# Token-row projections: the moving operand and the output of their matmuls walked in runs of 16 columns, alternately from two halves

## Time and profile before

| | |
|---|---|
| time before, median of 3 | 1237.65 us (1237.44 to 1240.28) |
| the profiled execution's own time | 1240.36 us |
| its span, first to last instruction | 1238.5 us |
| PE busy, matmuls | 1207.6 us (98%), 7597 |
| PE weight loads busy | 1015.8 us (82%) |
| DVE, ACT, POOL busy | 902.3, 638.7, 102.3 us |
| mean granted TensorE clock | 0.998 of full speed |

### The profile page before, as it was taken

One profiled execution on the slowest core, in us unless ns is written; L12 is line 12 of the kernel. 1 busy time (PEld: TensorE's weight loads), 2 busy tenths in 40 slices (PEclk: granted clock), 3 DMA queues, 4 the chain that ended last, 5 costly groups with the idle time before them and its releaser, 6 DMA issues.

```text
span 1238.5 us, 19034 instructions
## 1 busy us (share of the span) xinstructions
PE 1207.6 (98%) x7597; PEld 1015.8 (82%) x7597; DVE 902.3 (73%) x1463; ACT 638.7 (52%) x1034; POOL 102.3 (8%) x163
## 2 busy tenths in 40 slices
PE   7999999999999999999999999999999999999998
PEld 3566778887978888787999987988788787999986
DVE  7998867767598998687656555589998687665553
ACT  4334565575547665546434443556575535444441
POOL 6400011101000200201000001000200201000000
PEclk9999999999999999999999999999999999999999
DMA  7735566444565455355666664565445355556552
GB/s 253 210 103 178 200 210 191 152 130 154 162 202 166 151 160 188 124 179 170 208 187 187 187 190 155 174 217 171 154 153 180 139 174 170 188 195 196 191 194 75
DMA packets 71958, 215.68 MB, mean 174 GB/s; under 512 B 16256, under 2 KB 19744, under 8 KB 71744
## 3 DMA queue, kind: packets, MB, share of 16 engines
q1 hardware_dynamic: 65008, 206.37, 52.0%
q0 software_dynamic: 2112, 6.97, 1.9%
q10 hardware_dynamic: 4752, 1.14, 0.4%
HBM read 208.95 MB, written 3.15 MB: 171 GB/s over the span
## 4 chain that ended last, share of the span: by engine, by line
PE 82%; DVE 10%; ACT 5%; issue 2%; POOL 1%; DMA 0%; SPq 0%; DVEq 0%; POOLq 0%; ACTq 0%
PE acc L705 16%; PE acc L706 16%; PE acc L707 16%; PE acc L683 7%; PE acc L684 7%; PE acc L685 7%; PE acc L642 3%; DVE weights_lo L1780 2%; PE mixed L1020 1%; ACT junk L1284 1%; PE mixed L1117 1%; PE turned L760 1%; ACT weights_hi L1249 1%; DVE h_T L1810 1%; PE mixed L1004 1%
## 5 line engine op out<-in xcount | busy, mean ns | idle before, releaser
L1780 DVE TENSOR_TENSOR weights_lo<-weights_raw,weights_hi 128x1024 fp32r<-128x1024 f32 (+1 forms) x304 | 356.1, 1206 | 67.2 <-ACT weights_hi L1249 66.3
L1249 ACT ACTIVATE weights_hi<-weights_raw 128x1024 fp32r<-128x1024 f32 (+1 forms) x304 | 305.6, 1043 | 77.2 <-DMA weights_raw<-stream_dram 77.0
L705 PE MATMUL acc<-weights_hi,act_F_hi 128*128 128x512 f32 (+1 forms) x656 | 264.8, 404 | 4.2 <-DVE weights_lo L1780 2.5
L707 PE MATMUL acc<-weights_hi,act_F_lo 128*128 128x512 f32 (+1 forms) x656 | 256.7, 391 | 0.0
L706 PE MATMUL acc<-weights_lo,act_F_hi 128*128 128x512 f32 (+1 forms) x656 | 256.5, 391 | 0.0
L683 PE MATMUL acc<-act_F_hi,weights_hi 128*128 128x256 f32 x624 | 175.1, 281 | 0.0
L684 PE MATMUL acc<-act_F_hi,weights_lo 128*128 128x256 f32 x624 | 173.9, 279 | 0.0
L685 PE MATMUL acc<-act_F_lo,weights_hi 128*128 128x256 f32 x624 | 173.9, 279 | 0.0
L705 PEld LDWEIGHTS acc<-weights_hi,act_F_hi 128*128 128x128 f32 x656 | 123.6, 188 | 32.6 <-DVE weights_lo L1780 3.6
L707 PEld LDWEIGHTS acc<-weights_hi,act_F_lo 128*128 128x128 f32 x656 | 123.4, 188 | 26.8
L706 PEld LDWEIGHTS acc<-weights_lo,act_F_hi 128*128 128x128 f32 x656 | 123.7, 189 | 24.0
(11 more groups left out here) (351 smaller groups left out, 1969.6 us busy)
## 6 DMA issues: line engine op xcount, KB each, us to landing
weights_raw<-stream_dram SPq DMA_DIRECT2D x306, 512.0 KB, 3.6
weights_raw_more<-stream_dram SPq DMA_DIRECT2D x58, 512.0 KB, 3.6
gains<-rows_dram POOLq DMA_DIRECT2D x12, 512.0 KB, 4.7
weights_raw<-stream_dram SPq DMA_DIRECT2D x6, 416.0 KB, 3.1
weights_raw<-stream_dram SPq DMA_DIRECT2D x4, 384.0 KB, 3.9
x_T<-x_in_dram SPq DMA_DIRECT2D x4, 256.0 KB, 6.4
ssm_bc<-ssm_bc_dram SPq DMA_DIRECT2D x1, 1024.0 KB, 8.1
u_scratch<-u_T ACTq DMA_DIRECT2D x4, 256.0 KB, 6.2
```

Source lines behind the costliest of these rows:

```text
L705: pe.matmul(o, xh, wh, start=first and kk == 0, stop=False)
L707: i = pe.matmul(o, xl, wh, start=False, stop=last and kk == s["nk"] - 1)
L1249: act.activation(high(s, slice(0, n)), whole(s, slice(0, n)), ACT.Copy).then_inc(hi_made, 1)
L1780: dve.tensor_tensor(low(s, slice(0, n)), whole(s, slice(0, n)), high(s, slice(0, n)).bitcast(F32), ALU.subtract).then_inc(lo_made, 1)
```

## The change

In `tile_slot` the moving operands `wh` and `wl` and the output `o` get another access pattern, for all three matmuls. The w columns are seen as two halves (h) of n runs of 16 columns (c), and the order becomes n, h, c. For w = 512 TensorE is fed columns 0 to 15, 256 to 271, 16 to 31, 272 to 287, and so on, and writes each product column to the same column of PSUM as before. For w = 416 and 384 the halves are 208 and 192 columns wide. Data in memory, results and the instruction lists stay as they are otherwise.

```diff
@@ -702,6 +702,7 @@ def tile_slot(at, t):
                     wh, wl = (f(at, slice(kk * w, (kk + 1) * w)) for f in (high, low))
                     xh, xl = (f[:, k, t * P:(t + 1) * P] for f in (hi, lo))
                     o = acc[par][t][:, 0:w]
+                    wh, wl, o = (x.rearrange("p (h n c) -> p n h c", h=2, c=16) for x in (wh, wl, o))
                     pe.matmul(o, xh, wh, start=first and kk == 0, stop=False)
                     pe.matmul(o, xh, wl, start=False, stop=False)
                     i = pe.matmul(o, xl, wh, start=False, stop=last and kk == s["nk"] - 1)
```

## The result

The changed kernel is slower: median 1264.85 us (1263.36 to 1267.05, 4 runs) against 1237.73 us, ratio 1.022, interval 1.0208 to 1.0233. The forecast of no change (1237.7 us) was wrong by 27 us; the range, 1234 to 1278 us, held the time, and 0.32 had been given to slower. The profiled execution took 1265.93 us, with a span of 1264.1 against 1238.5: 25.6 us more.

What follows compares the result with a forecast made beforehand. The prediction took TensorE (PE) to bound the kernel. With zero added for reading and for writing in runs, the profiled execution stays at 1240.36 us, in terms of the median 1237.7 us; range 1234 to 1278 us.

Steps and rivals of the forecast that it cites:

- What bounds the kernel: TensorE, busy 98% of the span; a cost added to the touched matmuls arrives with a factor of 0.85 to 1.
- Writing in runs: PSUM side of the touched matmuls: taken as zero, assumed to behave like the reading side; no row shows it.
- rival 2: PSUM writes lose two columns' time or more per jump: 67 to 79 us, 1305 to 1317 us or above; chance 0.09.
- Reading in runs: Moving operands of the touched matmuls: taken as zero from line 900; 0.42 ns per jump kept for the range.
- Rival 1: Touched matmuls: each jump costs one column's time, at full rate only; 39.6 us of PE, 1271 to 1277 us; chance 0.14.
- Rival 3: Touched matmuls: a jump costs under 0.18 ns, which line 900 can't show; up to 17 us, 1242 to 1255 us; chance 0.09.
- Rival 4: Touched matmuls: the fixed 15 ns shrink to 2.6 ns; 34 to 40 us less, 1198 to 1204 us; chance 0.06 with parts.
- Rival 5: Touched matmuls' pattern is merged to the old one, time as forecast; counted within no change's 0.62.
- The range: Whole kernel, 1234 to 1278 us: the likeliest case, Rival 3 and Rival 1; rival 2 and nearly all of Rival 4 left out.

Runs made afterwards that it cites:

- e9: Kernel before, but the plain float32 matmuls in `whole_slot` (line 642) read and write in runs of 16 from the two halves; 1238.1 us, ratio 0.9994.
- e2: Kernel before, but only the output is written in runs of 16 to the two halves, reading in one piece; 1237.72 us, ratio 1.0001.
- e8: Kernel before, but only the output is written in pairs of columns, in turn to the two halves; 1239.26 us, ratio 1.0019.

## Why the prediction failed where it did

- *What bounds the kernel* was right: of the engines' busy times only PE's and its weight loads' changed, and 0.85 of PE's added time reached the median (27.1 of 31.8 us), at the lower end of the 0.85 to 1 expected.
- *Writing in runs* costs zero: right, and now shown for runs of 16 and of 2. No row stood behind it; it was an assumption that came true. So rival 2, the loss on the write side, is out. The Trainium skill's page "PSUM — Partial Sum Buffer" (section "Specifications (TRN2)") says that any non-contiguous pattern slows matmuls significantly; on this side the runs do not agree. They are in line with a sentence of the Trainium skill's page "Advanced Engine Details and Errata" (section "PSUM Cachelines"), which asks that every two consecutive elements be contiguous; writing single columns, the case that would test it, was not run.
- *Reading in runs* at zero is the step that failed: it cost 10.4 ns for each matmul with 512 columns. The zero was taken from line 900, which walks 8 runs of 16 for nothing, but at plain float32's rate. The text named this gap (room to hide 0.42 ns per jump) and then took the row's value all the same. e9 shows that plain float32 is no witness: the very same 31 jumps cost nothing in it, at 0.84 ns a column, and 10.4 ns in the touched lines, at 0.42.
- *Rival 1* (a price per jump at the full rate only) had the place and the condition right, and the size near: 10.4 / 31 = 0.34 ns per jump instead of 0.42, 1264.85 us instead of 1271 to 1277. Its law was wrong: with 512 columns 3 jumps cost nothing, 15 cost 0.47 ns each, 127 cost 0.17 each. So that the time came near its 1271 us is in part luck: at 31 jumps the price happened to lie near one column's time. Rival 3's bound of 0.18 ns, taken from line 900, was passed at the change's own 31 jumps.
- *Rival 4* was given little because "Nothing in the rows supports that the order of columns enters there", into the 15 ns. The order does enter: single columns in turn reduce them to 2.5 ns, near float32's 2.6, in 1208 us. In the changed kernel it did not come.
- *Rival 5*, a pattern merged to the old one, is out by the distances alone.
- *The range* held because the gap of the reading row had been carried into it as 34 to 40 us; 27 came. That is a hedge that held; the mechanism behind the likeliest value, reading for nothing, was wrong.

## What to carry to other kernels

A row that shows an access pattern for nothing vouches for it only at its own rate and in its own type: ask whether the row ran slow enough to hide the cost, and weigh that gap in the likeliest value, not only in the range. Where the same matmul runs thousands of times on a bound engine, take its distance from start to start less its columns; what is left may belong to how the operand is read. Here, at one column per 0.417 ns, a moving operand of 512 columns was as fast in runs of 128 as in one piece (229.6 ns), slower in runs of 4 to 32 (236.7 to 250.7 ns) and fastest in single columns (215.8 ns); an output written in runs of 16 or in pairs cost nothing.

## What the runs showed that was not expected

- Reading single columns in turn from two places 256 columns apart is faster than reading neighbours: 215.8 against 229.6 ns. Whether that comes from a step other than one between neighbours or from the distance, and why runs of 4 to 32 are worse than both ends, stays open; no run tells it apart. Runs of 2 were not read.
- Single distances differ in their evenness. In the kernel before, dense neighbours with 512 columns were 225 to 237 ns apart, in many stretches 226, 229 and 232 over and over; in the changed kernel 2733 of 2778 were 240 exactly, and with single columns all but one were 215 or 216. So the 15 ns are a mean, not a constant.
- The traces speak against other traffic as the cause of those 15 ns. Before, the distance was 229.0 ns where DVE and ACT were each idle for at least half of it and 229.7 where both were busy for more than half; with fewer than four DMA transfers under way it was 229.6, with 16 or more 229.4.
- The mean cost is on a grid for three run lengths: 568, 576 and 584 columns' times with 512 columns for runs of 32, 16 and 8 (236.7, 240.0, 243.4 ns times 2.4), and 424, 432 and 440 with 384 columns (176.9, 180.1, 183.3 ns). Runs of 4 leave it (250.7 ns is 602 with 512 columns, 188.4 ns is 452 with 384).
- The untouched lines 683 to 685 come in two distances. Two stretches of the kernel before, each 24 matmuls long:

```profile
699.84 0.28 PE L683 MATMUL acc<-act_F_hi,weights_hi_more 128*128 128x256 f32 x1
...
702.66 0.28 PE L683 MATMUL acc<-act_F_hi,weights_hi_more 128*128 128x256 f32 x1
...
1109.79 0.28 PE L684 MATMUL acc<-act_F_hi,weights_lo 128*128 128x256 f32 x1
...
1112.51 0.28 PE L684 MATMUL acc<-act_F_hi,weights_lo 128*128 128x256 f32 x1
```

117.5 ns and 113.3 ns. Which of the two a stretch has differs between executions: over all 2496 the mean was 115.3 ns before, 113.7 in e2, and 116.7 in e8. In e8 that is 2496 x 1.4 ns = 3.5 us of the 5.0 by which the span of its profiled execution (1243.5 us) is longer than 1238.5. A comparison of two single executions can thus be off by some 4 us that the change has no part in, and the medians go first. The cause wasn't sought.
